# A two-layer encoder trunk on one core: three extra weight places filled twice, pre-mixer norms copied in their own order, and attention units issued behind the reload

## The reference

```
for i in range(2):
    h = rms_norm(x, norm1_g[i])
    x = x + (conformer_conv(h, ...) if i == 0 else diff_attention(h, ...))
    h = rms_norm(x, norm2_g[i])
    x = x + hierarchical_moe(h, ...)
```

## Time and profile before

| quantity | value |
|---|---|
| runs shown | 1612.61, 1613.57, 1616.12 us, median 1613.57 |
| profiled execution | 1612.3 us |
| its span, first to last instruction | 1610.4 us |
| TensorE busy | 1333.8 us, 83% of the span |
| VectorE, ScalarE, GpSimd busy | 443.5, 331.5, 268.9 us |
| mean granted TensorE clock | 0.976 of full |
| moved by DMA | 473.32 MB, mean 294 GB/s |

### The profile page before, as it was taken

One profiled execution on the slowest core, in us unless ns is written; L12 is line 12 of the kernel. 1 busy time (PEld: TensorE's weight loads), 2 busy tenths in 40 slices (PEclk: granted clock), 3 DMA queues, 4 the chain that ended last, 5 costly groups with the idle time before them and its releaser, 6 DMA issues.

```text
span 1610.4 us, 20667 instructions
## 1 busy us (share of the span) xinstructions
PE 1333.8 (83%) x8048; PEld 764.1 (47%) x8048; DVE 443.5 (28%) x957; ACT 331.5 (21%) x638; POOL 268.9 (17%) x370
## 2 busy tenths in 40 slices
PE   6998898997777777773799999999997777777773
PEld 3443456654444444441466665656564444444441
DVE  1798445110101001001444454436110110101012
ACT  3665221000000000000444444422000000000000
POOL 3788000211111111100000000000211111111100
PEclk9999999999999999997799999999999999999997
DMA  8413128899999999999400400426899999999995
GB/s 295 152 52 157 52 86 344 330 423 423 426 423 426 424 423 424 423 425 361 161 1 1 157 1 14 196 118 241 335 426 424 424 425 424 423 424 425 423 419 225
DMA packets 73197, 473.32 MB, mean 294 GB/s; under 512 B 16198, under 2 KB 20294, under 8 KB 38840
## 3 DMA queue, kind: packets, MB, share of 16 engines
q1 hardware_dynamic: 60760, 443.67, 67.2%
q0 software_dynamic: 10080, 16.35, 2.7%
q10 hardware_dynamic: 2304, 12.58, 2.0%
HBM read 465.93 MB, written 23.33 MB: 304 GB/s over the span
## 4 chain that ended last, share of the span: by engine, by line
DMA 44%; PE 43%; DVE 6%; ACT 3%; POOL 3%; issue 1%; SPq 0%; ACTq 0%; POOLq 0%; DVEq 0%
DMA ring<-in_moe_w 39%; PE banks L1441 9%; PE banks L1457 7%; PE banks L1557 6%; PE banks L1586 4%; PE banks L1358 3%; POOL scratch L542 2%; DMA area<-in_moe_w 2%; PE banks L1265 2%; DVE banks L927 2%; PE banks L1344 2%; PE banks L1646 2%; PE banks L1601 1%; PE banks L1285 1%; DMA area<-y_dram 1%
## 5 line engine op out<-in xcount | busy, mean ns | idle before, releaser
L1441 PE MATMUL banks<-ring,scratch 128*64 128x256 f32 x3904 | 445.2, 381 | 108.2 <-DMA ring<-in_moe_w 104.2
L1441 PEld LDWEIGHTS banks<-ring,scratch 128*64 128x64 f32 x3904 | 291.4, 137 | 281.7 <-DMA ring<-in_moe_w 114.7
L1457 PE MATMUL banks<-ring,scratch 128*64 128x512 f32 x992 | 229.9, 604 | 74.4 <-DMA ring<-in_moe_w 72.7
L1098 DVE COPY scratch<-banks 128x256 f32<-128x256 f32 x65 | 27.6, 425 | 816.9 <-PE banks L1449 816.9
L1457 PEld LDWEIGHTS banks<-ring,scratch 128*64 128x64 f32 x992 | 77.7, 138 | 187.7 <-issue 179.2
L734 ACT ACTIVATE scratch<-banks 128x256 f32<-128x256 f32 x65 | 25.0, 384 | 527.4 <-PE banks L1441 524.2
L1557 PE MATMUL banks<-hT,ring 128*128 128x512 f32 x256 | 119.9, 613 | 0.8 <-DVE hT L881 0.8
L1265 PE MATMUL banks<-hT,ring 128*128 128x512 f32 x256 | 114.2, 606 | 0.8 <-DVE hT L881 0.8
L572 POOL COPY at_out<-rows_out 128x1 int32 (+1 forms) x58 | 10.6, 183 | 610.8 <-ACT scratch L738 610.8
L738 ACT ACTIVATE scratch<-banks 128x512 f32<-128x512 f32 x65 | 38.8, 597 | 350.4 <-PE banks L1457 350.4
L542 POOL TENSOR_TENSOR scratch<-scratch 128x512 f32<-128x512 f32 x77 | 98.0, 1274 | 23.0 <-ACT scratch L701 13.1
(11 more groups left out here) (226 smaller groups left out, 1206.9 us busy)
## 6 DMA issues: line engine op xcount, KB each, us to landing
ring<-in_moe_w SPq DMA_DIRECT2D x184, 2048.0 KB, 27.2
area<-in_moe_w SPq DMA_DIRECT2D x8, 2048.0 KB, 11.8
ring<-in_attn_w_qkv SPq DMA_DIRECT2D x6, 2048.0 KB, 18.2
area<-y_dram ACTq DMA_DIRECT2D x8, 1024.0 KB, 8.8
hT<-in_moe_w SPq DMA_DIRECT2D x3, 2048.0 KB, 16.7
ring<-in_conv_w_in SPq DMA_DIRECT2D x4, 1024.0 KB, 11.8
ring<-in_conv_w_in SPq DMA_DIRECT2D x2, 2048.0 KB
ring<-in_conv_w_out SPq DMA_DIRECT2D x2, 2048.0 KB
```

The lines of the kernel that those rows point to most:

```text
L1441: last = mm(bank[2 + s][q * SLOTS:(q + 1) * SLOTS, k * 256:(k + 1) * 256], xeT[s][:, c % 4, c // 4, :], wc[:, c, q * 256:(q + 1) * 256], s ...
L1457: last = mm(bank[6 + s][q * SLOTS:(q + 1) * SLOTS, :], hidT[s][:, j % 2, j // 2, :], w2c[:, j, q * 512:(q + 1) * 512], start=j == 0, stop= ...
```

## The change

- `MOE_UNITS`, the number of units that go through the ring in an expert stage, falls from 92 to 89, because three go to extra places that are filled a second time: w2 of expert 4 to area3, w1 of expert 6 to area2, w3 of expert 6 to hT. SyncE waits for the product that read the place before (`up` 3, `y` 2, `w1_used` 4). All later ring units move by three numbers; from unit 18 on the releases that SyncE waits for are again those it waited for before with the same expert's weights.
- TensorE's steps 5 and 6 take these three units from the extra places; steps 6 to 9 are written out, and the loop runs from 10.
- Attention units 1 and 2 are issued after the wait for the reload, with 3 to 5; unit 0 stays where it was.
- In norms 0 and 2 ScalarE's copy writes xn in x's own channel order. TensorE's transposes for them read every eighth column of xn.

```diff
--- before.py
+++ after.py
@@ -59,7 +59,7 @@
 FAR = 2048
 LAYERS = 2
 MIX_UNITS = (6, 8)
-MOE_UNITS = 3 * EXPERTS - 4
+MOE_UNITS = 3 * EXPERTS - 7
 FIRST = (0, MIX_UNITS[0] + MOE_UNITS)
 ROUTE_LOADS = 16 * (12 + 4 * LAYERS)
 LAMBDA_INIT = 0.8 - 0.6 * math.exp(-0.3 * 1)
@@ -382,11 +382,24 @@
                 down_to_ring(9, 3, up, 2)
                 to_ring(10, w1_of(5), y, 1)
                 to_ring(11, w3_of(5), w1_used, 3)
-                with sp.Fori(1, EXPERTS // 2 - 3) as i:
+                sp.wait_ge(up, 3)
+                load_unit(halves_of(extra_units[0]), w2_of(4), extra_loaded[0])
+                to_extra(1, w1_of(6), y, 2)
+                to_extra(2, w3_of(6), w1_used, 4)
+                for s in range(2):
+                    down_to_ring(12 + 3 * s, 5 + s, y, 3 + s)
+                    to_ring(13 + 3 * s, w1_of(7 + s), w1_used, 5 + s)
+                    to_ring(14 + 3 * s, w3_of(7 + s), up, 5 + s)
+
+                def loop_units(s, e):
+                    down_to_ring(3 * s, e, y, e - 1)
+                    to_ring(3 * s + 1, w1_of(e + 2), w1_used, e + 1)
+                    to_ring(3 * s + 2, w3_of(e + 2), up, e + 1)
+
+                with sp.Fori(3, EXPERTS // 2 - 3) as i:
                     for s in range(2):
-                        down_to_ring(3 * s, i * 2 + (s + 2), y, i * 2 + (s + 1))
-                        to_ring(3 * s + 1, w1_of(i * 2 + (s + 4)), w1_used, i * 2 + (s + 3))
-                        to_ring(3 * s + 2, w3_of(i * 2 + (s + 4)), up, i * 2 + (s + 3))
+                        loop_units(s, i * 2 + (s + 1))
+                loop_units(0, EXPERTS - 5)
                 down_to_ring(MOE_UNITS - 8, EXPERTS - 4, y, EXPERTS - 5)
                 to_ring(MOE_UNITS - 7, w1_of(EXPERTS - 2), w1_used, EXPERTS - 3)
                 to_ring(MOE_UNITS - 6, w3_of(EXPERTS - 2), up, EXPERTS - 3)
@@ -462,16 +475,13 @@
             def first_qkv():
                 sp.wait_ge(done["up_ready"], EXPERTS - 1)
                 qkv_unit(0)
-                sp.wait_ge(done["up_ready"], EXPERTS)
-                qkv_unit(1)
-                qkv_unit(2)
 
             moe_weights(0, [(glu_ready, 2), (glu_ready, 4)] + [(glu_ready, 8)] * 2 + [(mix_ready, 4), (mix_ready, 8)], first_qkv)
             sp.wait_ge(done["y_ready"], EXPERTS)
             sp.wait_ge(moe_over, 1)
             for t in range(NT):
                 sp.wait_ge(y_loaded[t], 16)
-            for n in (3, 4, 5):
+            for n in range(1, 6):
                 qkv_unit(n)
             sp.wait_ge(qk_ready, 8)
             for n in range(2):
@@ -661,9 +671,12 @@
             def normalise(n, t):
 
                 act.wait_ge(rstd_done, 4 * n + t + 1)
-                a.activation(xn[:, t, :].rearrange("p (h j q) -> p h j q", h=2, j=4),
-                             x_res[:, t, :].rearrange("p (q h j) -> p h j q", h=2, j=4), ACT.Copy,
-                             scale=rstd[:, t:t + 1]).then_inc(xn_done, 1)
+                if n in N_MOE:
+                    a.activation(xn[:, t, :].rearrange("p (h j q) -> p h j q", h=2, j=4),
+                                 x_res[:, t, :].rearrange("p (q h j) -> p h j q", h=2, j=4), ACT.Copy,
+                                 scale=rstd[:, t:t + 1]).then_inc(xn_done, 1)
+                else:
+                    a.activation(xn[:, t, :], x_res[:, t, :], ACT.Copy, scale=rstd[:, t:t + 1]).then_inc(xn_done, 1)
 
             for t in range(NT):
                 norm_stats(N_PRE[0], t)
@@ -1250,7 +1263,7 @@
                     if m >= 2:
                         pe.wait_ge(xt_taken, m - 1)
                     for j in range(4):
-                        src = x_res[:, t, 4 * h + j:4 * h + j + 1017:8] if raw else xn[:, t, (4 * h + j) * P:(4 * h + j + 1) * P]
+                        src = (x_res if raw else xn)[:, t, 4 * h + j:4 * h + j + 1017:8]
                         last = nc.tensor.transpose(bank[6 + h][:, j * P:(j + 1) * P], src, ident[:])
                     last.then_inc(xt_ready, 1)
 
@@ -1467,8 +1480,8 @@
                     n = n0 + r
                     return unit(n), unit_loaded[n % RING], i * 16 + 16 * (n // RING + 1)
 
-                def in_extra(k):
-                    return extra_units[k], extra_loaded[k], 16 * (l + 1)
+                def in_extra(k, again=0):
+                    return extra_units[k], extra_loaded[k], 16 * ((l + 1) if k == 3 else 2 * l + 1 + again)
 
                 def up_step(e, s, w1, w3):
 
@@ -1506,11 +1519,15 @@
                 step(2, 0, in_ring(5), in_extra(0), in_extra(1), first=True)
                 step(3, 1, in_extra(2), in_extra(3), in_ring(6))
                 step(4, 0, in_ring(7), in_ring(8), in_ring(9))
-                step(5, 1, in_ring(10), in_ring(11), in_ring(12))
-                with pe.Fori(0, EXPERTS // 2 - 4) as i:
+                step(5, 1, in_ring(10), in_ring(11), in_extra(0, 1))
+                step(6, 0, in_extra(1, 1), in_extra(2, 1), in_ring(12))
+                for e in (7, 8, 9):
+                    r = 13 + 3 * (e - 7)
+                    step(e, e % 2, in_ring(r), in_ring(r + 1), in_ring(r + 2))
+                with pe.Fori(0, EXPERTS // 2 - 6) as i:
                     for q in range(2):
-                        r = 13 + 3 * q
-                        step(i * 2 + (6 + q), q, in_ring(r, i), in_ring(r + 1, i), in_ring(r + 2, i))
+                        r = 22 + 3 * q
+                        step(i * 2 + (10 + q), q, in_ring(r, i), in_ring(r + 1, i), in_ring(r + 2, i))
                 up_step(EXPERTS - 2, 0, in_ring(MOE_UNITS - 7), in_ring(MOE_UNITS - 6))
                 hid_T(m, 1, EXPERTS - 2)
                 rows_step(EXPERTS - 1, 1)
```

## The result

The changed kernel took 1585.28 us in the median of 4 runs (1583.95 to 1586.34), beside 1614.12 for the kernel before (1612.61 to 1616.12, 4 runs). The ratio is 0.982, with a 95% interval of 0.9803 to 0.9837: 28.8 us faster, where 25.2 were forecast from the profiled execution. The profiled executions are 27.2 us apart (1612.3 and 1585.1).

A forecast was written before the change was run, and what follows sets the result against it. Bound: weight stream in expert stages, compute chain in mixer stages. 15.9 + 4.3 + 2.3 + 3.25 - 0.6 = 25.15 us off 1612.3 gives 1587.2, stated as 1588; range 1584.4 less 1.4 for runs, up to 1601.

The forecast's parts named there:

- The second filling: Expert stages: three extra places filled again keep the weight stream going, saving 15.9 us (bounds 0 to 15.9).
- its pauses: Idle weight stream once per expert stage, until the third down-projection frees a place: 8.1 us layer 0, 7.8 layer 1.
- the margins: Place freed by the sixth down-projection is ready before the stream needs it: 3.4 us in layer 0, 3.5 layer 1.
- rival 1: Expert stages: the pause is only put off, to unit 18; gain 9.2 us, time 1603, chance 0.12.
- The first norm: Before the convolution layer's mixer: four shorter ScalarE copies in series start TensorE's products 4.3 us earlier.
- rival 2: Both pre-mixer norms gain nothing: first weights, and VectorE's queue in layer 1, set the starts; 1594 us, chance 0.12.
- The second norm: Before attention in layer 1: shorter ScalarE copies interleaved with VectorE's combining save 2.3 us (bounds 1.1 and 4.3).
- the Square's wait: Norm before attention: the last Square starts late because the third copy holds ScalarE; 0.9 us to be saved.
- The strided transposes: Pre-mixer transposes: TensorE picking every eighth column costs 0.3 us per layer, 0.6 in all (bounds 0 and 1.2).
- The attention units: End of layer 0: units 1 and 2 behind the reload shorten the last scatter by 3.25 us, at cost 0.
- rival 3: Attention start: units come late, sharing the stream five deep; TensorE stands 10 us, time 1598, chance 0.05.
- Rival 4: Attention: TensorE's clock stays at its lower level, making the kernel slower, 1617 at 60 us; chance 0.05.

The follow-up runs named there:

- the delay: Changed kernel plus nine spare products between TensorE's steps 1 and 2: 1615.87 us with no place filled twice, 1594.86 with three, 1589.12 with four.

## Why the prediction was right, point by point

**The second filling** gave what its pauses said. The stages won 8.81 and 6.82 us, 15.6 together, where 8.1 + 7.8 were forecast. The count of places (two are enough) and the delay (paid in full without places, absorbed to within 0.7 us of the margins with them) show the mechanism, and rival 1, the pause put off, is out: no low window stands near 340, and a fourth place changes nothing. The split was less exact than the sum. Layer 1 won 1 us less than its pause. In the changed kernel TensorE took 1120.01 - 1096.28 = 23.7 us over its first steps there, 2 more than before; with the old places that would have lengthened the pause. With the other parts in place (none against three places), the stages are 8.5 and 9.6 us apart, and whole runs about 19: 1604.6 against 1585.3. A part of TensorE's loss is paid even without a pause: the kernels that had no pause and took 23.7 to 24.1 us over these steps (the changed one, two and four places, the old norms, all units behind the reload) have second stages of 464.7 to 466.2 us; the two with spare products between the transposes took 21.5 and have 463.6 and 463.7. That is about the 1 us that layer 1 lacks. No window is low there, and what passes it on is not shown. So the worth of the filling is not one number. It is the pause, and that grows with each us that TensorE loses ahead of its third down-projection.

**The first norm** won 3.96 of 4.3. The copy took 1.15 us, not 1.06 as sized by the Square's row, and 4 x (2.14 - 1.15) is just those 3.96. Timeline of the changed kernel:

```profile
15.10 1.15 ACT L679 ACTIVATE area<-x_res,small 128x1024 f32<-128x1024 f32 x1 [0.23 <-DVE small L887]
...
19.06 13.52 PE L1278 MATMUL banks<-hT,ring 128*128 128x512 f32 x27 [0.78 <-DVE hT L894]
```

The releaser of the first products is still VectorE, not a DMA, so the weights were there and rival 2 is out. **The second norm** won 2.8, where 2.3 less 0.3 was forecast: the strided loads cost nothing (below), the last copy gave 0.99 and the Square's wait 0.88. The remaining 0.9 is in how VectorE's and ScalarE's queues interleave (from the reload's first tile to the last combination 13.59 us for 14.54), which I had sized at 0.3.

**The strided transposes** were forecast to cost 0.6 us, and cost nothing. The transposes' weight loads at line 1267 of the changed kernel:

```profile
L1267 PEld LDWEIGHTS banks<-ident,area x64: 185/226/231, 8.1 to 760.3; 128*128 128x128 f32 x64
```

The contiguous ones of the kernel with the old norms:

```profile
L1264 PEld LDWEIGHTS banks<-ident,area x64: 180/230/231, 9.1 to 766.4; 128*128 128x128 f32 x64
```

226 ns against 230 at the lower clock, and a tile's 8 loads took 1.57 us either way. The step that failed is the scaling of the upper clock's ratio (188 to 142) to the lower one. The ratio itself was thin ground: the route's products (line 1404) load contiguous columns of the same xn, also at the upper clock, and their loads of 128x128 took 192 ns in the median, so that the stride makes 142 into 188 is not shown. The Trainium skill ("SBUF — State Buffer", section "Door 1: The DMA port swizzle") states that each access which crosses to a new 16-byte line pays a penalty. ScalarE's copy agrees, 2.14 us strided against 1.15 packed; TensorE's weight loads at 1.2 GHz don't show it.

**The attention units** were mis-sized by a term that I hadn't written. The scatter gave its 3.3 us, and the reload's first tile another 1.6 (6.41 to 4.83): the units' packets were still in flight when the reload began, at 753.59. Finer windows of the kernel before would have shown it, with DMA shares of 0.60, 0.49 and 0.34 in the 3 us before 754; the changed kernel has 0.00 to 0.09 in the 3 us before its reload. The units were in time, so rival 3 is out: between 755 and 880 us no attention product waited for a DMA, the first ones only 0.8 us for VectorE. Rival 4 is out too: the clock left its lower level some 4.8 us into the first products (0.50 to 765, 1.00 from 767), as before (0.50 to 786, 1.00 from 788).

**The remainder.** In the convolution layer the first products were 1.03 us shorter (15.66 for 16.69) and the 32 records before the experts 1.63 longer, at a granted clock of 0.57 from 244 to 248 (5.20 for 3.57). The stretch lost 0.08, so another 0.5 was won between them that I haven't traced. The first of these looks like a clock that rose sooner, but the clock column reads 1.00 from the start of the span in both kernels. It is the records that say so: weight loads there last 0.34 us until 22.5 and then 0.19, as in attention, where the column goes from 0.50 to 1.00.

**Sum.** The span shrank by 27.1 where 25.15 was forecast. The misses are +0.7 and -1.0 in the stages, +1.6 at the reload and +0.8 in the second norm, and -0.2 in the rest. The range held them all, but that the total lies within 2 us is in part luck: the misses have both signs, and one of them is the reload term that was not in the sum.

## What to carry to other kernels

Where a stream is the limit, look for its idle windows, name the event that ends each, and count how many units of buffer would carry it over: a third place was needless here and two were enough. A pause that ends with a compute event also charges the stream for every delay of that engine, so buffers beyond the count are worth nothing as long as that engine is on time and something when it is late (a fourth place: nothing, and about 3 us with TensorE held up). Move loads that nobody needs yet behind the short transfers that everybody waits for, and count both of these when a scatter is followed by a reload.

## What the runs showed of the hardware that I had not expected

Spare products in gaps of 0.65 to 2.2 us between short transposes brought TensorE's granted clock from 0.50 to 0.92 over the second and third tile's transposes, and it fell back to 0.50 over the last one, before the products. Even so the first products left the lower level after about 1 us instead of 4.8, and the whole was 4 us of 1585 shorter. In the changed kernel and most of its variants the clock also fell to its lower level within busy stretches that follow a short wait, for 1.6 or 1.7 us a time: 5.20 against 3.57 us for the same 32 matmul records after TensorE had been busy for 0.97 of 2 us, and 5.28 against 3.58 for a down-projection after 0.23 of 2 us. Where it falls differs from kernel to kernel, and whether it can be kept up there as well was not tried.

The granted clock's column can read 1.00 where the records are those of the lower level; so it does in the changed kernel's first 22 us, where weight loads last 0.34 us and later 0.19.
